# Low parts of 49 weight entries made by accumulating DMAs of GpSimd instead of VectorE subtractions

## What is computed

```
x = x + merged @ w_mix_out                       # 2048 x 2048
u = square(relu(rmsnorm(x) @ w_ff1))             # 2048 x 8192
x = x + u @ w_ff2                                # 8192 x 2048   (the "ff2" groups)
x = rmsnorm(x)                                   # end of the first block
x = x + concat(attention, pool) @ w_out_2        # second block
y = conv_b + sum_i conv_w[i] * shift(h @ w_up_2) # 2048 x 2*5632
x = x + (silu(gate) * val) @ w_down_2            # 5632 x 2048   (the "down" groups)
```

## Time and profile before

| | us |
|---|---|
| median of 3 runs | 2369.18 |
| lowest, highest | 2367.63, 2369.34 |
| the profiled execution's own time | 2369.1 |
| its span in the trace | 2367.3 |
| TensorE busy | 2362.3 (100%), 12510 matmuls |
| VectorE busy | 1787.1 (75%) |
| ScalarE busy | 1292.2 (55%) |
| GpSimd busy | 0.2 |
| DMA, mean | 191 GB/s, 452 MB |

### The profile page before, as it was taken

How to read it: one execution, slowest core, us unless ns; L and a number is a source line. 1 busy time by engine, 2 the same in 40 slices (tenths; PEclk the granted TensorE clock), 3 DMA queues, 4 the chain that set the end, 5 groups by cost and what they waited for, 6 DMA issues and landing times.

```text
span 2367.3 us, 31012 instructions
## 1 busy us (share of the span) xinstructions
PE 2362.3 (100%) x12510; PEld 2023.8 (85%) x12510; DVE 1787.1 (75%) x1964; ACT 1292.2 (55%) x1512; POOL 0.2 (0%) x4
## 2 busy tenths in 40 slices
PE   9999999999999999999999999999999999999999
PEld 8888888888888888888888888888888888888887
DVE  5575666666877967967968777888778788897888
ACT  5454454554656555556556566556555555555554
POOL 0000000000000000000000000000000000000000
PEclk9999999999999999999999999999999999999999
DMA  7556556665665675665665555556555655565655
GB/s 253 163 176 200 158 196 193 192 191 171 203 203 171 223 231 171 214 197 184 213 195 190 185 187 169 169 178 198 184 187 186 205 177 188 187 221 187 189 173 183
DMA packets 238044, 452.17 MB, mean 191 GB/s; under 512 B 16570, under 2 KB 20780, under 8 KB 237772
## 3 DMA queue, kind: packets, MB, share of 16 engines
q1 hardware_dynamic: 237147, 449.07, 58.8%
q10 hardware_dynamic: 752, 1.12, 0.1%
HBM read 446.46 MB, written 3.67 MB: 190 GB/s over the span
## 4 chain that ended last, share of the span: by engine, by line
PE 99%; DVE 1%; DMA 0%; ACT 0%; issue 0%; ACTq 0%; DVEq 0%
PE PS L696 42%; PE PS L698 21%; PE PS L729 11%; PE PS L731 11%; PE PS L730 11%; PE PS L658 0%; PE PS L625 0%; PE PS L646 0%; PE PS L635 0%; PE PS L563 0%; DVE WL L1335 0%; DMA VR<-in_g_mix 0%; PE PS L708 0%; PE PS L647 0%; PE PS L626 0%; PE PS L552 0%
## 5 line engine op out<-in xcount | busy, mean ns | idle before, releaser
L1335 DVE TENSOR_TENSOR WL<-RAW,WH 128x1024 fp32r<-128x1024 f32 (+1 forms) x844 | 991.0, 1193 | 431.9 <-ACT WH L856 429.4
L696 PE MATMUL PS<-XHL,WH 128*128 128x512 f32 x3968 | 1248.2, 396 | 0.0
L856 ACT ACTIVATE WH<-RAW 128x1024 fp32r<-128x1024 f32 (+1 forms) x845 | 859.4, 1032 | 659.0 <-PE PS L698 455.1
L698 PEld LDWEIGHTS PS<-XHL,WL 128*128 128x128 f32 x3968 | 745.4, 188 | 176.0
L698 PE MATMUL PS<-XHL,WL 128*128 128x256 f32 x3968 | 779.8, 278 | 0.0
L696 PEld LDWEIGHTS PS<-XHL,WH 128*128 128x128 f32 x3968 | 605.1, 189 | 2.1 <-issue 1.0
L729 PE MATMUL PS<-WH,MHL 128*128 128x512 f32 x915 | 356.9, 390 | 0.0
L731 PE MATMUL PS<-WH,MHL 128*128 128x512 f32 x915 | 356.1, 389 | 0.0
L730 PE MATMUL PS<-WL,MHL 128*128 128x512 f32 x915 | 356.0, 389 | 0.0
L731 PEld LDWEIGHTS PS<-WH,MHL 128*128 128x128 f32 x915 | 171.7, 188 | 35.9
L730 PEld LDWEIGHTS PS<-WL,MHL 128*128 128x128 f32 x915 | 171.8, 188 | 35.1
(11 more groups left out here) (226 smaller groups left out, 1613.8 us busy)
## 6 DMA issues: line engine op xcount, KB each, us to landing
RAW<-in_w_ff SPq DMA_DIRECT2D x256, 512.0 KB, 4.2
RAW<-in_w_in SPq DMA_DIRECT2D x224, 512.0 KB, 3.9
RAW<-in_w_up SPq DMA_DIRECT2D x176, 512.0 KB, 4.5
RAW<-in_w_down SPq DMA_DIRECT2D x88, 512.0 KB, 4.3
RAW<-in_w_mix_out SPq DMA_DIRECT2D x32, 512.0 KB, 4.2
RAW<-in_w_out SPq DMA_DIRECT2D x32, 512.0 KB, 4.2
RAW<-in_w_conv_out SPq DMA_DIRECT2D x16, 512.0 KB, 3.6
RAW<-in_w_attn_out SPq DMA_DIRECT2D x16, 512.0 KB, 4.2
```

What stands on the lines that cost most here:

```text
L696: mm(PS[:, b + p.banks[j], :], h[:, k, j * P:(j + 1) * P], x[:, kc, :], start=st, stop=False)
L698: t = mm(PS[:, b + p.banks[j], 0:T], l[:, k, j * P:(j + 1) * P], x[:, kc, 0:T], start=False, stop=en)
L856: act(high, raw, AF.Copy).then_inc(*own.made(hi, i))
L1335: tt(low, raw, high.bitcast(f32), sub).then_inc(*own.made(lo, i))
```

## The change

In the ff2 and down groups, 49 entries are chosen, always the second entry of an ordinary step, with at least two entries to the last chosen one and seven to the one before that (`added`). For such an entry VectorE no longer makes the low part. ScalarE reads RAW a second time, with a scale of -1, and writes the negated rounded value into WLX, a new pair of buffers used in turn (`negative`, before the split of the entry two ahead of the chosen one). GpSimd waits for that and issues a DMA that reads the same 512 KB of weights again from HBM and adds them onto WLX, so that WLX holds value - high. TensorE's first matmul of that entry waits for the DMA (`low_landed`) and for the high part. The buffer in RAW is free once the high part is made.

Memory for WLX comes from a new place for AS (inside TC). BIAS shares memory with WLX and is therefore loaded some 180 units later, and the mask is added at the start of item ("Q", 0) of the second block. GF is loaded where it was.

```diff
+APART = 7
+ADDED, ADDED_FROM = ("ff", "down"), 1
...
-            AXH = sb("AXH", [P, 3, 4, P], f32r, c=c)
-            AXL = sb("AXL", [P, 3, 4, P], f32r, c=c)
-            AS = sb("AS", [P, 4, P], c=c)
-            sb("QK2pad", [P, 512], c=c)
+            AXH = sb("AXH", [P, 4, 4, P], f32r, c=c)
+            AXL = sb("AXL", [P, 4, 4, P], f32r, c=c)
             GF = sb("GF", [P, D], c=c)
+            WLX = sb("WLX", [P, 2, UNIT], f32r, c=c)
...
+        AS = TC[:, :, 2:2 + P]
...
+            if buf is WL and e in added:
+                return WLX[:, added[e] % 2, 0:per * n].rearrange("p (k n) -> p k n", k=per)
...
+        added, last_two = {}, [-APART, -APART]
+        for it in items:
+            for n, st in enumerate(it.steps):
+                if it.args["u"][0] in ADDED and not st.seven:
+                    for ent in st.ents[ADDED_FROM:]:
+                        if ent - last_two[0] >= APART and ent - last_two[1] >= 2:
+                            added[ent] = len(added)
+                            last_two = [last_two[1], ent]
+        BIAS_UNIT = ents[item_of["ff2", 3, 2].parts[0].ent][1] + AHEAD + NR + 4
...
+            if e in added:
+                raw_free[u] = hi, e
+            elif what == "unit":
                 raw_free[u] = lo, e
...
+        def gpsimd(e):
+            own = Own(e, None)
+            for i, n in added.items():
+                own.wait_ge(*negated[i])
+                e.dma_start(wview(WL, i), units[ents[i][1]][0], accum_op=add).then_inc(s_low[n % 2], 16)
...
-                            own.wait_ge(*lo[ent])
+                            if ent in added:
+                                own.wait_ge(*hi[ent])
+                                own.wait_ge(*low_landed(ent))
+                            else:
+                                own.wait_ge(*lo[ent])
...
+                    if i + 2 in added:
+                        negative(i + 2)
...
+            def negative(i):
+                u, n = ents[i][1], added[i]
+                own.wait_ge(*landed(u))
+                if n >= 2:
+                    own.wait_ge(*used[added_ents[n - 2]])
+                if i == first_added_mix:
+                    own.wait_ge(*used[item_of["conv", 3].end])
+                if i == first_added_wo:
+                    own.wait_ge(*masked[2, 1])
+                act(wview(WL, i), raw_view(u), AF.Copy, scale=-1.0).then_inc(*own.made(negated, i))
...
-                    own.wait_ge(*hi[i])
-                    tt(low, raw, high.bitcast(f32), sub).then_inc(*own.made(lo, i))
+                    if i not in added:
+                        own.wait_ge(*hi[i])
+                        tt(low, raw, high.bitcast(f32), sub).then_inc(*own.made(lo, i))
```

More of the change, by code:

```diff
@@ L389, in build @@
         s_id, s_gm, s_vr, s_const, s_rel = (sem(n) for n in ("s_id", "s_gm", "s_vr", "s_const", "s_rel"))
+        s_low = [sem("s_low0"), sem("s_low1")]
         s_er, s_wp, s_gf = sem("s_er"), sem("s_wp"), sem("s_gf")
@@ L402, in build @@
             signals("used used_half gm_up vec_up rel_up turned spread_up logf_up run_up scores probs_up mix_up norm_up"))
-        hi, x_hi, part_hi, sum_hi, copied, squared, root, gate, tap, exps, probs, placed, softplus, cr_hi, square_hi, pair1, rooted, act_step = (
-            signals("hi x_hi part_hi sum_hi copied squared root gate tap exps probs placed softplus cr_hi square_hi pair1 rooted act_step"))
+        hi, x_hi, part_hi, sum_hi, copied, squared, root, gate, tap, exps, probs, placed, softplus, cr_hi, square_hi, pair1, rooted, negated, act_step = (
+            signals("hi x_hi part_hi sum_hi copied squared root gate tap exps probs placed softplus cr_hi square_hi pair1 rooted negated act_step"))
         lo, t13_made, t_made, x_lo, square_lo, summed, summing, left, evacuated, scaled, multiplied, tapped, mean, column, diagonal, row = (
@@ L443, in pieces, with low_landed @@
             return raw, high, low
+        item_of = {it.key: it for it in items}
+        added, last_two = {}, [-APART, -APART]
[6 more added lines that the diff above has]
+                            last_two = [last_two[1], ent]
+        added_ents = list(added)
+        BIAS_UNIT = ents[item_of["ff2", 3, 2].parts[0].ent][1] + AHEAD + NR + 4
+        added_before_bias = max((e for e in added if e < item_of["ff2", 3, 2].parts[0].ent), default=None)
+        first_added_mix = min((e for e in added if e < item_of["ff", 0, 0].parts[0].ent), default=None)
+        first_added_wo = min((e for e in added if e > item_of["Q", 0].end), default=None)
+        def low_landed(e):
+            n = added[e]
+            return s_low[n % 2], 16 * (n // 2 + 1)
         raw_free = {}
         for e, (what, u) in enumerate(ents):
-            if what == "unit":
+            if e in added:
+                raw_free[u] = hi, e
+            elif what == "unit":
                 raw_free[u] = lo, e
@@ L494, in build @@
         rel_all, er_all = 48, 16 * 16
-        item_of = {it.key: it for it in items}
         BIAS_AFTER = ents[item_of["ff", 1, 0].parts[0].ent][1] + AHEAD - 1 + NR
@@ L524, in sync @@
                 if i == BIAS_AFTER:
+                    own.wait_ge(*used[branches_end])
+                    e.dma_start(GF[:], io["g_final"].rearrange("(a n) -> a n", a=1).to_broadcast([P, D])
+                                ).then_inc(s_gf, 16)
+                if i == BIAS_UNIT:
                     own.wait_ge(s_er, er_all)
                     own.wait_ge(*used[branches_end])
+                    if added_before_bias is not None:
+                        own.wait_ge(*used[added_before_bias])
                     e.dma_start(BIAS[:], bass.AP(ERD.tensor, ERD.offset + P - 1, [[8 * 384 - 1, P], [384, 8], [1, T]])
                                 ).then_inc(s_wp, 16)
-                    e.dma_start(GF[:], io["g_final"].rearrange("(a n) -> a n", a=1).to_broadcast([P, D])
-                                ).then_inc(s_gf, 16)
             for g in range(2):
@@ L1062, in pair_sums @@
                     own.wait_ge(*used[sum_used[i]])
-                act(AXH[:, i], AS[:], AF.Copy).then_inc(*own.made(sum_hi, (u, i)))
+                act(AXH[:, i], AS, AF.Copy).then_inc(*own.made(sum_hi, (u, i)))
                 free["TA"] = summed, (u, i)
@@ L1650, in pair_sums @@
                 own.wait_ge(*sum_hi[u, i])
-                tt(AXL[:, i], AS[:], AXH[:, i].bitcast(f32), sub).then_inc(*own.made(summed, (u, i)))
+                tt(AXL[:, i], AS, AXH[:, i].bitcast(f32), sub).then_inc(*own.made(summed, (u, i)))
             def sums_x(it):
@@ L1950, in vector @@
                     e.memset(TC[:, :, 0:2], 0.0).then_inc(*own.made())
-                elif it.key == ("ff", 3, 1):
+                elif it.key == ("Q", 0):
                     chain()
@@ L1954, in vector @@
                     tt(BIAS[:], BIAS[:], over4(M, 8), add).then_inc(*own.made())
-                elif it.key == ("Q", 0):
                     chain()
@@ L1986, in vector @@
             work.flush()
-        for engine in (tensor, vector, scalar, sync):
+        for engine in (tensor, vector, scalar, gpsimd, sync):
             engine(Counting())
@@ L2006, in _ @@
             vector(nc.vector)
+        @block.gpsimd
+        def _(eng):
+            gpsimd(nc.gpsimd)
         @block.tensor
```

## The result

The changed kernel takes **2391.93 us** (median of 4 runs, 2389.08 to 2394.88), against 2369.2 us for the kernel before (4 runs, 2367.63 to 2369.34) on the same chip: ratio 1.0098, 95% interval 1.008 to 1.0115. It is slower by 22.7 us. That lies inside the range of the prediction (2368 to 2402) and outside the likeliest case (2369 to 2373.6). It is rival 1.

What follows compares the result with a forecast made beforehand. It took TensorE, at full clock and one pace, to bound the kernel. Stops of 1.0 us less 0.3 us of VectorE relief gave +0.7 us on 2369.1 us, forecast 2370 us; eight-in-ten range 2368 to 2402.

Steps and rivals of the forecast that it cites:

- likeliest case: Whole kernel: no change that can be measured, 2370 us, own range 2369 to 2373.6 us, chance 0.56.
- rival 1: At chosen entries the accumulation lands late and TensorE stops: slower, 4.4 us over at 8.1 us landing, 2402 us at 10.2; chance 0.28.
- signs of being wrong: WLX landing over 8 us with repeated stops behind two seven steps; ScalarE's split waiting for DMA in step 4; pace not 0.227 us.
- rival 3: VectorE's or DMA's work slows TensorE's matmuls, so the change makes the kernel faster by over 4.7 us; chance 0.03.
- VectorE's relief: Taking 49 subtractions, 60 us of busy time, from VectorE gives back at most 0.3 us at the end.
- BIAS cost nothing: BIAS's later load and the mask's addition before Q0 cost nothing; 2.3 us once if the cover were gone.
- The rooms: Time from negated copy's end to TensorE's first matmul: 6.2 us first down group, 7.8 behind two seven steps, 8.3 ff2 step 4.
- estimate of L: Time from negated copy's end until the DMA has landed, by the skill's two figures: 2.0 + 2.4 = 4.4 us, zero stops.
- term L: Time from negated copy's end until the DMA has landed: 2.6 + 3.1 + 0.9 + 0.4, taken as 7.1 us, ends 4.2 and 10.2.
- its own formula: TensorE's stops: landing time less 6.2 once, less 7.8 nine times, less 8.3 four times, where positive, plus 0.1; 1.0 us.
- rival 2: Loads into RAW come late because accumulations share their engines, four stops in step 4 of ff2 groups: +4 to +12 us; chance 0.13.
- the cover of the copies: ScalarE's 49 added copies, 52 us, lie beside TensorE's work; only a pushed split in the first down group costs 0.1 us.

## Why the prediction was right and wrong

**By the range and by the forecast.** The time lies in the range only because that reached to the far end of rival 1, which had a chance of 0.28; the forecast itself, no change, did not come true. The prediction's own signs of being wrong did: a median of 8.3 us from issue to landing (over 8) and repeated stops behind two seven steps.

**Right.** TensorE's pace stayed 0.227 us, so neither VectorE's nor DMA's work slows matmuls (rival 3 falls). BIAS cost nothing, as costed. VectorE's relief was worth nothing (2367.58 us with 19 entries, 2367.73 us with all 49 subtractions gone and nothing to wait for). The engine time of an accumulation, two reads, was put at 3.1 us and is 3.07. The rooms were close: 7.9 where I had 7.8, 8.1 for 8.3, 6.5 for 6.2. Of the 21 places with 9.7 to 10.6 us of room 18 stayed free, as I had put it up to the end of my range; the other three stopped for 0.83, 0.51 and 0.32 us, TensorE starting the entry 9.5 to 11.2 us after the copy's end. There two loads went out with the accumulation, and the accumulation before it was still under way on the same queue (it landed 3.2 to 4.6 us after this copy's end), which the prediction had no term for.

By the Trainium skill (Collectives: The Full Stack, § The bandwidth ceiling) an adding transfer has half the rate because it reads two sources. The trace has 3.07 us against 1.57 for a load and 1.84 for a plain DMA on the same queue, so between 1.7 and 2 times. The estimate of L that the prediction made with it, 4.4 us, is under the shortest landing seen (5.8).

**Wrong: the term L, taken as 7.1 us; at the 8 places that decide it was 9.3.** The prediction's step was "it finds on average 0.59 x 1.57 = 0.9 us of another load ahead". Where no load goes out with the accumulation it is even too much: there the landing takes about 6.3 us from the copy's end, and 2.6 + 3.1 + 0.4 = 6.1. At the places that decide it is far too little. Loads go out when ScalarE and VectorE free a buffer of RAW, and the copy stands among the same steps, so at the 8 places behind two seven steps two loads (at one place a load and two stores) are issued in the same microsecond as the accumulation, and it begins 1.3 to 2.7 us later and then has company. It landed 8.9 to 10.0 us after the copy's end there (9.3 on average). Counted to TensorE's start, some 0.14 us later, that is 9.0 to 10.2 (9.4 on average), 8.7 in step 4 of the ff2 groups and 7.6 in the first down group's step 4. With these in its own formula the prediction gives 1.4 + 8 x 1.6 + 4 x 0.4 + 0.1 - 0.3 = 15.6 us, and 1.7 us for the three of the 21: 17.3, against 16.8 us measured in the 16 stops. The ninth place with 7.8 us of room is the last row of the table of neighbours: no load, no stop. So rooms, places and mechanism held, and one term was an average where two streams are in step. The prediction had the right row in hand: it held against rival 1 that two loads of 1 MB "were issued right behind each other and so held each other up", and that is what happens to the accumulation.

The other 5.9 us of the 22.7 are what stops bring with them (slower matmuls behind them, half clock) and the items' starts; the formula had no term for these.

By the Trainium skill (DMA: Bandwidth & Descriptors, § Queues, rings and completion order), quoted in the prediction, each engine takes turns between its queues packet by packet. The accumulation did not get its turn at once: its first packet came 3.5 to 4.9 us after the copy instead of 2.2. The prediction used the rule against rival 2 alone; taken for rival 1 it would have misled as well.

**Wrong: the cover of the copies.** ScalarE's 52 us were costed at nothing because they lie beside TensorE's work. That is true of the work (2367.73 us with copies that wait for nothing) and not of the wait that the copy brings. Rival 2 had a copy waiting for its unit, but only in step 4 of the ff2 groups, and only through the accumulations' share of the engines. In fact the copies of step 4 did not wait at all. Others waited, 28.5 us in 13 places: above all those in step 6 of the same groups (1.5 to 1.9 us) and those of the chosen entries that follow the 8 behind two seven steps (1.8 to 3.0 us). In the run with copies and no accumulation they waited 21.1 us, and that cost 9.3 us. The prediction named no row for what is queued behind the waiting copy on ScalarE: splits whose units were in, and the copy of PB out of PSUM. Within the change this cost is hidden behind the other; it decides as soon as one tries to mend the first.

**Not foreseen: the clock.** I had no term for a stop beyond its own length. Behind the longest stop of the change TensorE ran at half clock (last section), 1.6 us.

## What to carry to other kernels

To cost a new transfer, look at what is issued in the same microsecond at the place that decides, not at the mean share of the DMA engines: what frees a buffer for the other stream can stand among the same instructions as what starts yours, as here. An instruction that is put early on an in-order engine carries its wait along, so ask what stands behind it and is ready; here the early copy was free only when it had nothing to wait for. And relief for an engine that TensorE doesn't wait for was worth nothing, 60 us of it.

## What the runs showed of the hardware

- **An accumulating DMA of 512 KB** from GpSimd took 1.20 us to issue (a plain one 0.72), 3.07 us of the DMA engines (1.84), and 5.8 / 8.3 / 11.4 us (least, median, most) from issue to landing (3.9 / 5.8 / 8.5).
- **Between queues.** Counted from the start of GpSimd's issue (0.3 us after the copy's end), the accumulation's first packet came after 1.9 to 2.0 us in the changed kernel where no other load was issued near it, or where the nearest was issued 1.05 us or more before or 1.2 us or more after that start. With one or two loads (or two stores) issued from 0.9 us before to 0.7 us after it, the first packet came after 3.2 to 4.7 us. Whether VectorE was busy all that time or for 0.7 of it made no difference (1.9 us both).
- **The granted clock of TensorE behind a stop.** The row of windows (us busy of TensorE, its weight loads, VectorE, ScalarE, GpSimd; granted clock; DMA share; GB/s) of the changed kernel around the longest stop, TensorE having begun again at 2090.41:

```profile
2090.50:2095.00 4.50, 4.50 (x13) 3.55 (x14) 3.59 (x5) 2.31 (x3) 0.00 (x0) 0.62 1.09 295
2095.00:2100.00 5.00, 5.00 (x23) 4.11 (x23) 4.93 (x5) 2.12 (x2) 0.00 (x0) 1.00 0.81 306
```

TensorE's timeline of the changed kernel in the same stretch shows the distance of matmuls go from 0.23 to 0.43 us:

```profile
2090.41 0.47 PE L765 MATMUL PS<-WH,MHL 128*128 128x512 f32 x1 [2.06 <-DMA WLX<-in_w_down]
...
2091.18 0.40 PE L765 MATMUL PS<-WH,MHL 128*128 128x512 f32 x1
2091.41 0.56 PE L766 MATMUL PS<-WLX,MHL 128*128 128x512 f32 x1
2091.77 0.63 PE L767 MATMUL PS<-WH,MHL 128*128 128x512 f32 x1
2092.20 0.63 PE L765 MATMUL PS<-WH,MHL 128*128 128x512 f32 x1
```

That is 1.2 instead of 2.4 GHz. Over the runs, of three stops of 2.23 or 2.24 us one was followed by it, those of 2.46 and 2.51 us were, and all 16 of 2.9 us or more were. It cost 1.4 to 3.0 us each time, on top of the stop.

What stays open: why the first packets wait behind the loads (whether in GpSimd's part or in the DMA engines), and the 1.0 us of the table that have no place.
